# Moving the Gelu evacuation of the RG-LRU stage from the middle of a head to the end of the head before

## The reference

```
xc = centred_depthwise_conv(lx, w, bias)            # lx = h @ w_in[x columns]
ga = xc @ lru_w_a + b_a ;  gi = xc @ lru_w_i + b_i  # per block of 128, per direction
log_a = -8 * softplus(-lam) * sigmoid(ga);  a = exp(log_a)
b = sqrt(-expm1(2 * log_a)) * (sigmoid(gi) * xc)
h_t = a_t h_{t-1} + b_t                             # forward, and backward over the flipped sequence
y_lru = (h_fwd + h_bwd) * gelu(ly)                  # ly = h @ w_in[y columns]
```

## Time and profile before

| what | value |
|---|---|
| median of 3 runs | 3127.97 us (3125.83 to 3128.83) |
| profiled execution | 3128.83 us, span 3127.0 us |
| TensorE busy | 2897.6 us, 93% |
| VectorE busy | 1786.0 us, 57% |
| ScalarE busy | 1163.8 us, 37% |
| GpSimd busy | 767.6 us, 25% |
| mean granted TensorE clock | 0.963 |
| first sigmoid of head 0, last VectorE instruction of the stage | 92.42 us, 467.80 us |

### The profile page before, as it was taken

The page is one execution under the profiler, slowest core; times in us unless marked ns, Lnnn a source line. Parts: engine busy times, 40 slices in busy tenths (PEclk is TensorE's granted clock), DMA queues, the critical chain, the costliest instruction groups (busy, mean ns, idle before and its releaser), DMA issues. The chain is left out here.

```text
span 3127.0 us, 41861 instructions
## 1 busy us (share of the span) xinstructions
PE 2897.6 (93%) x17008; PEld 2795.7 (89%) x17008; DVE 1786.0 (57%) x2397; ACT 1163.8 (37%) x1761; POOL 767.6 (25%) x363
## 2 busy tenths in 40 slices
PE   7999968999999599799996989999999999999996
PEld 6999967878988499699986989999999999999995
DVE  6788881234344396799995443677763332223237
ACT  2789883234344322244444110101571122211224
POOL 0233311100100021544542333333212112111220
PEclk9999988989999699899998999999999999999998
DMA  5111101000100134344435353634211111111111
GB/s 215 52 64 60 64 19 63 31 26 29 42 32 21 54 98 171 123 118 126 130 98 166 112 191 122 205 132 164 84 34 41 48 41 41 42 47 41 41 44 65
DMA packets 111164, 257.82 MB, mean 82 GB/s; under 512 B 20944, under 2 KB 54736, under 8 KB 110736
## 3 DMA queue, kind: packets, MB, share of 16 engines
q1 hardware_dynamic: 100912, 214.26, 21.0%
q10 hardware_dynamic: 10080, 41.18, 3.5%
HBM read 199.01 MB, written 56.37 MB: 82 GB/s over the span
## 5 line engine op out<-in xcount | busy, mean ns | idle before, releaser
L2539 PE MATMUL bank<-yhi,mrg_hi 128*128 128x384 f32 x1560 | 526.3, 337 | 3.3 <-POOL mrg_lo L2482 1.8
L2539 PE MATMUL bank<-ylo,mrg_hi 128*128 128x384 f32 x1560 | 522.9, 335 | 0.0
L2539 PE MATMUL bank<-yhi,mrg_lo 128*128 128x384 f32 x1560 | 522.8, 335 | 0.0
L2482 POOL TENSOR_TENSOR mrg_lo<-mrg_raw,mrg_hi 128x1024 fp32r<-128x1024 f32 x69 | 169.5, 2457 | 678.5 <-ACT mrg_hi L2641 678.5
L2506 PE MATMUL bank<-yhi,mrg_hi 128*128 128x384 f32 x864 | 293.0, 339 | 39.9 <-POOL mrg_lo L167 24.3
L2539 PEld LDWEIGHTS bank<-yhi,mrg_hi 128*128 128x128 f32 x1560 | 293.9, 188 | 6.9 <-POOL mrg_lo L2482 2.6
L2539 PEld LDWEIGHTS bank<-ylo,mrg_hi 128*128 128x128 f32 x1560 | 293.8, 188 | 1.2 <-issue 0.3
L2539 PEld LDWEIGHTS bank<-yhi,mrg_lo 128*128 128x128 f32 x1560 | 293.8, 188 | 0.0
L2506 PE MATMUL bank<-ylo,mrg_hi 128*128 128x384 f32 x864 | 290.8, 337 | 0.0
L2506 PE MATMUL bank<-yhi,mrg_lo 128*128 128x384 f32 x864 | 290.7, 336 | 0.0
L1720 PE MATMUL bank<-hhi,s_hi 128*128 128x384 f32 x768 | 265.1, 345 | 22.5 <-POOL s_lo L180 19.3
(11 more groups left out here) (398 smaller groups left out, 6413.3 us busy)
## 6 DMA issues: line engine op xcount, KB each, us to landing
mrg_raw<-in_mlp_units SPq DMA_DIRECT2D x64, 512.0 KB, 3.5
s_raw<-in_s_units SPq DMA_DIRECT2D x32, 512.0 KB, 4.6
mrg_scr<-in_w_ada_rows SPq DMA_DIRECT2D x32, 512.0 KB, 3.6
mid_gates<-gate ACTq DMA_DIRECT2D x24, 576.0 KB, 3.1
gt<-mid_gates SPq DMA_DIRECT2D x24, 576.0 KB, 3.8
gla_raw<-in_gla_units SPq DMA_DIRECT2D x25, 512.0 KB, 3.7
lru_raw<-in_lru_units SPq DMA_DIRECT2D x24, 512.0 KB, 3.9
x<-in_x_t SPq DMA_DIRECT2D x16, 576.0 KB, 9.8
```

The source lines that it names most:

```text
L2482: pool.tensor_tensor(WLO[SLOT[u]], S.raw[u % 2], WHI[SLOT[u]].bitcast(F32), ALU.subtract).then_inc(S.split_done, 1)
L2539: mm = pe.matmul(out, wt[SLOT[u]][:, w], r[:, k, band_cols(b)], start=(k == first and y == 0), stop=(k == last and y == 2))
```

## The change

`evac_y` of a head is called at the end of the head before it, between the roots and the Sigmoid warm call that already stands there. The call in the middle of the head goes away, and with it the second warm call. Head 0's own `evac_y(0)`, ahead of the loop, stays.

```diff
                         if b == 0:
                             unit_hi(2 * i + 3)
-                        if b == 1 and i:
-                            evac_y(i)
-                            act.activation(warm[:], tiny[:], ACT.Sigmoid)
                     unit_hi(2 * i + 4)
                     gates_hi(i + 1)
...
                     roots(i)
                     if i + 1 < LBLK:
+                        evac_y(i + 1)
                         act.activation(warm[:], tiny[:], ACT.Sigmoid)
```

## The result

| | median | range |
|---|---|---|
| before, shared runs | 3126.9 us | 3117.7 to 3128.8 (4 runs) |
| changed | 3157.5 us | 3149.7 to 3159.2 (4 runs) |
| ratio | 1.0097 | 95% interval 1.0075 to 1.0120 |

The changed kernel is slower by about 1%. The direction and the mechanism were forecast. The size was not: 22.6 us was forecast and some 30 measured, and 3157.5 us lies above the range of 3144 to 3156.

The account below looks back on a forecast made before the run. TensorE was taken to set the pace, with a ScalarE loop close behind; 2.57 + 21.2 + 2.36 - 3.97 + 0.4 = +22.6 us on 3127.97 gave 3150.6 us, range 3144 to 3156 for 8 in 10.

Parts of the forecast that it names:

- What bounds the stage: RG-LRU stage: TensorE sets the pace at 31.38 us a head; ScalarE's first sigmoid leaves the fourth gate product 0.18 us slack.
- Steps 1 and 2: Block removed from mid-head takes 3.97 us but gains 0.21; block added at head's end costs 2.57, without wait or cover.
- Step 3: A head through both engines: 14.48 + 16.77 + 2.57 = 33.82 us, above TensorE's 31.38, so the fourth gate product stalls.
- Step 4: Sum over the stage: +2.57 head 0, +21.2 heads 1 to 9, +2.36 head 10, -3.97 and +0.4 head 11: +22.6 us.
- the clock: TensorE's granted clock was taken to stay 1.00 through head 10; a fall in head 11 was priced at 0.
- The rival: Clock falls in each of some 11 TensorE gaps, about 3 us each, priced at 26: 3177 us; chance 0.04.
- the bound of +3: Head 11's gap ahead of the fourth product grows to about 4.7 us; if the clock falls there, up to +3 us.
- Nothing else moves: Step 5: y bands, VectorE's combine and SP's order cause no delay; behind the stage's barrier the rest shifts as a whole.

Follow-up runs that it names:

- addload: Kernel before, nothing moved, with a Gelu table load and one-column call added at the end of heads 0 to 10; ratio 1.0043.
- g345: Changed kernel with each head's twelve gate products and sigmoids cut 3, 4, 5 between the x bands instead of 4, 4, 4; ratio 0.9993.
- fill: Changed kernel with unread matmuls ahead of the fourth gate product, 12 in heads 1 to 10 and 26 in head 11; ratio 1.0057.
- g345_before: Kernel before, evacuation still in the middle of the head, with the gate products cut 3, 4, 5; ratio 0.9998.
- longgap: Changed kernel with one more table load and one-column Exp call, 1.49 us, at the end of heads 0 to 10; ratio 1.0189.
- fill4: Changed kernel with 4 unread matmuls ahead of the fourth gate product of heads 1 to 11; ratio 1.0063.
- shift: Changed kernel with 40 unread matmuls ahead of the fourth gate product of head 1 alone; head 2 33.66 us, heads 5 and 8 35.22 and 35.11.
- tail: Kernel before with the evacuation moved for head 11 alone, to the end of head 10; ratio 0.9993.
- copy_evac: Changed kernel with y evacuated by Copy instead of Gelu in heads 1 to 11, so without that table load; ratio 1.0022.
- best: Changed kernel, gates cut 3, 4, 5, head 11's evacuation behind its own roots, decays' wait for the combine behind two Exp calls; ratio 0.9990.

## Why the prediction was right in kind and wrong in size

- *What bounds the stage.* Right. TensorE's pace with a loop through ScalarE close behind: addload measured the slack at 0.24 us (read 0.18), and g345 showed that the loop closes at the fourth product.
- *Steps 1 and 2, the removed and the added block.* Right. The block of 2.57 us starts behind the roots without a wait, and the removed one was worth little outside the last head.
- *Step 3, a head of 33.82 us.* Measured 33.65 in the changed kernel and 33.66 in fill. The difference of 0.17 us lies between the warm call and the first sigmoid: 161.97 - 161.44 = 0.53 us, and 123.67 - 122.97 = 0.70 behind head 0 of before, from which the term was taken. ScalarE's timeline of before has the warm call here.

```profile
122.97 0.20 ACT L557 ACTIVATE lru_warm<-lru_tiny 128x1 f32<-128x1 f32 x1
```

- *Step 4, the sum of +22.6.* At full clock it is +21.1, measured by fill: 2.4 for 2.57 in head 0, 9 x 2.2 for 9 x 2.36, 2.35 for 2.36, and -3.6 for -3.57 in head 11. With it alone the time would be some 3149 us, inside the range.
- *The step that failed is the clock.* "Against: the gap of 2.14 us in head 11 is of the same size as the new ones and the granted clock behind it is 1.00." One gap behind which the clock held was taken as a rule for ten. In each of two traces of the changed kernel it fell behind 3 of 10 such gaps, and in g345_before it fell at the very place that was the witness. The rival had a chance of 0.04 and a price of 26 us as all or nothing; the truth lay between, at 3 x 1.55. Its price of 3 us a fall was too high as well: a fall cost 1.55 here, and 2.4 in longgap. Nor was 0 right for head 11: its gap became 4.70 us as computed, the bound of +3 was on paper, and it cost 1.7.
- *Head 0.* Its order up to the fourth product is untouched, and its clock held in the trace of before. In the two traces of the changed kernel it fell, before any moved instruction ran, and cost 2.2 us. It also fell in fill4, g345, shift, addload, g345_before and tail, the last with head 0 as in before, and it held in fill, copy_evac, longgap and best. So nothing that the edit moved decides whether it falls, and what does stays open. What a fall there costs does depend on the kernel: 0.14 us in tail, 2.2 in the changed one. It was in neither the sum nor the bounds.
- *Nothing else moves.* Right for the stages behind the barrier as far as their scatter of 12 us lets one see.

So the size follows: 21 us of stalls, net of what head 11 gains, 6.4 of falls behind the new and the longer gaps, 2.2 of a fall in head 0. That is 29.5 in the stage, and 27 to 31 in the medians. What decides behind which 2.08 us gap the clock falls stays open.

## What to carry to other kernels

Where two engines hand banks back and forth, look for the instruction that waits first and count what stands ahead of its releaser; an engine's idle time elsewhere in the loop is no cover. The cure was not the cheaper block but another place for the waiting product: g345 keeps the added block and loses the stall. Price every new TensorE gap of some 2 us with a share of falls of the clock, from several gaps of the trace and not from one, and compare stages from one barrier to the next before whole times.

## What was not expected of the hardware

- Behind gaps of 2.08 us the granted clock fell in some heads and not in others, in the same ones (2, 5, 8) in two executions; behind gaps of 0.6, 1.05 and 1.38 us in none of heads 1 to 10; behind gaps of 3.62 us in all ten.
- A fall cost more behind the longer gap: 1.55 us at 2.08; at 3.62 it was 2.4 in heads 2 to 10 and 1.5 in head 1.
- With extra matmuls whose result nobody reads in the gaps, the clock held, and heads 1 to 11 were 6.2 us shorter together.
